# Value pages two per block, and the last sequence's early pages on a semaphore of their own

## What is computed

```
def paged(cache_l):
    rows = cache_l[page_table]
    return rows.reshape((n_seq, n_pages * cache_l.shape[1]) + cache_l.shape[2:])
past = (paged(cache_moba_k[l]), paged(cache_moba_v[l]), paged(cache_fox_k[l]), paged(cache_fox_v[l]), paged(cache_fox_logf[l]), state_hgrn[l])
...
p = jax.nn.softmax(s.reshape(B, H, qb, -1), axis=-1).reshape(s.shape)
return jnp.einsum('bhqnk,bhqnkd->bhqd', p.astype(vs.dtype), vs)
```

## Time and profile before

| | us |
|---|---|
| time, median of 3 executions | 1693.34 |
| lowest and highest of them | 1688.63, 1697.64 |
| profiled execution: span from first to last instruction | 1707.6 |
| TensorE busy in it | 1613.0 |
| POOL busy in it | 181.4 |
| TensorE's waits in line 1924 for key pages | 20.3 |

### The profile page before, as it was taken

One profiled execution on the slowest core, in us unless ns is written; L12 is line 12 of the kernel. 1 busy time (PEld: TensorE's weight loads), 2 busy tenths in 40 slices (PEclk: granted clock), 3 DMA queues, 4 the chain that ended last, 5 costly groups with the idle time before them and its releaser, 6 DMA issues. The chain is left out here.

```text
span 1707.6 us, 35370 instructions
## 1 busy us (share of the span) xinstructions
PE 1613.0 (94%) x13333; PEld 1498.8 (88%) x13333; DVE 1042.5 (61%) x1768; ACT 674.3 (39%) x987; POOL 181.4 (11%) x345
## 2 busy tenths in 40 slices
PE   6999999999898699999999999999898878999998
PEld 6999999976676599999999999999566657999997
DVE  6666557766485566665566665566656735666654
ACT  4333333445453553333343333425555444433322
POOL 0000000022454100000000000000235520000000
PEclk9999999999898899999999999999899988999999
DMA  6444446556677444444444444654677863544444
GB/s 200 149 150 152 152 137 146 127 179 221 208 240 235 146 149 150 150 155 138 148 156 151 153 142 141 161 136 125 214 221 228 257 202 94 180 147 147 141 146 138
DMA packets 282235, 282.34 MB, mean 165 GB/s; under 512 B 43022, under 2 KB 271046, under 8 KB 281990
## 3 DMA queue, kind: packets, MB, share of 16 engines
q1 hardware_dynamic: 266338, 234.28, 44.9%
q0 software_dynamic: 14464, 46.48, 8.5%
q10 hardware_dynamic: 1316, 0.03, 0.1%
HBM read 274.34 MB, written 6.40 MB: 164 GB/s over the span
## 5 line engine op out<-in xcount | busy, mean ns | idle before, releaser
L1707 PE MATMUL PS<-xh,whi 128*128 128x320 f32 x1840 | 576.1, 313 | 13.5 <-DVE xl L1021 7.3
L1707 PE MATMUL PS<-xl,whi 128*128 128x320 f32 x1840 | 569.4, 309 | 0.0
L1707 PE MATMUL PS<-xh,wlo 128*128 128x320 f32 x1840 | 569.3, 309 | 0.0
L687 ACT ACTIVATE whi<-raw 128x2048 fp32r<-128x2048 f32 (+1 forms) x181 | 330.9, 1829 | 565.1 <-PE PS L1707 560.2
L1012 DVE TENSOR_TENSOR wlo<-raw,whi 128x2048 fp32r<-128x2048 f32 (+1 forms) x181 | 395.2, 2185 | 237.2 <-ACT whi L687 235.5
L1707 PEld LDWEIGHTS PS<-xh,whi 128*128 128x128 f32 x1840 | 346.3, 188 | 16.7 <-DVE wlo L1012 10.7
L1707 PEld LDWEIGHTS PS<-xh,wlo 128*128 128x128 f32 x1840 | 346.2, 188 | 1.5
L1707 PEld LDWEIGHTS PS<-xl,whi 128*128 128x128 f32 x1840 | 346.1, 188 | 0.0
L1707 PE MATMUL PS<-hh,whi 128*128 128x320 f32 x704 | 217.7, 309 | 0.0
L1707 PE MATMUL PS<-hl,whi 128*128 128x320 f32 x704 | 217.5, 309 | 0.0
L1707 PE MATMUL PS<-hh,wlo 128*128 128x320 f32 x704 | 217.5, 309 | 0.0
(11 more groups left out here) (271 smaller groups left out, 1842.0 us busy)
## 6 DMA issues: line engine op xcount, KB each, us to landing
raw<-in_ffn_w_gate SPq DMA_DIRECT2D x45, 1024.0 KB
raw<-in_ffn_w_up SPq DMA_DIRECT2D x45, 1024.0 KB
raw<-in_ffn_w_down SPq DMA_DIRECT2D x32, 1024.0 KB
key_pages<-in_cache_moba_k SPq DMA_DIRECT2D x128, 192.0 KB, 3.2
raw<-in_w_in SPq DMA_DIRECT2D x46, 512.0 KB
value_pages<-in_cache_moba_v POOLq DMA_DIRECT2D x118, 192.0 KB, 3.6
key_pages<-in_cache_fox_k SPq DMA_DIRECT2D x128, 160.0 KB, 4.1
value_pages<-in_cache_fox_v POOLq DMA_DIRECT2D x118, 160.0 KB, 4.3
```

Of the source, the lines that this page charges most:

```text
L687: act.activation(whi[s][:, 0:nk, 0:w], raw[s][:, 0:nk, 0:w], ACT.Copy).then_inc(hi_done[s], 1)
L1707: last = te.matmul(out, w[wslot][r, kt, cols], x[r, at, :], start=start and n == 0 and m == 0, stop=stop and n == len(ktiles) - 1 and m == 2)
```

## The change

Value pages are issued in other blocks, in the same queue and with the same transfers.

- Sequence 0: pages 0 and 1 are issued behind `add_past(3)` and `add_past(4)`, before the loop; the other six in the loop's steps 2, 3 and 4, two each. Before, all eight were issued ahead of the loop, with `add_past(2)` to `add_past(5)` between them.
- Sequences 1 to 6: two pages in each of the steps 4q + 1 to 4q + 4. Before, four pages in each of the steps 4q + 2 and 4q + 3.
- The five early pages of sequence 7: one in each of the steps 11 to 15, on the new semaphore `late_values_in`. Before, three in step 24 and two in step 25, on `v_in`.
- `values(7)` waits for all five at once; `values(q)` of the others counts only its own loads.

```diff
+        late_values_in = sem("late_values_in")
...
-                        load_page(DB - 1, pg, late_pages[:, pg, :], v_in[pg])
+                        load_page(DB - 1, pg, late_pages[:, pg, :], late_values_in)
...
-                for i, first, count in ((2, 0, 1), (3, 1, 1), (4, 2, 2), (5, 4, 2)):
+                add_past(2)
+                add_past(3)
+                for i, first, count in ((4, 0, 1), (5, 1, 1)):
                     load_values(0, first, count)
                     add_past(i)
-                load_values(0, 6, 2)
                 pool.memset(a_blocks[:, :, :], 0.0).then_inc(products_cleared, 1)
                 for i in range(BLOCKS):
                     q, n = divmod(i, NBLK)
...
-                    if n >= 2 and 1 <= q < DB - 1:
-                        load_values(q, 4 * (n - 2), 4)
-                    if n < 2 and q == DB - 2:
-                        load_late_values(3 * n, 3 - n)
+                    if 2 <= i < 5:
+                        load_values(0, 2 * i - 2, 2)
+                    if NBLK < i <= NBLK * (DB - 1):
+                        load_values((i - 1) // NBLK, 2 * ((i - 1) % NBLK), 2)
+                    if NH <= i < NH + LATE:
+                        load_late_values(i - NH, 1)
                     if n == 2 and q == DB - 1:
                         load_values(q, LATE, NPG - LATE)
...
+                    if q == DB - 1:
+                        te.wait_ge(late_values_in, (L + 1) * LATE * 32)
                     for pg in range(NPG):
                         late = q == DB - 1 and pg < LATE
                         page = (late_pages if late else value_pages)[:, pg, :]
-                        loads = min(q + 2, DB) if pg < LATE and q >= DB - 3 else q + 1
-                        te.wait_ge(v_in[pg], (L * DB + loads) * 32)
+                        if not late:
+                            te.wait_ge(v_in[pg], (L * (DB - 1 if pg < LATE else DB) + q + 1) * 32)
```

## The result

The changed kernel takes 1680.97 us in the median of 5 runs (1677.13 to 1681.54), the kernel before beside it 1696.41 (1688.63 to 1697.64): a ratio of 0.9895, 95% interval 0.9869 to 0.9921. It is faster, by that ratio by 17.8 us (13.4 to 22.2); the two medians lie 15.4 apart. The prediction said 29 and 1664 us. The time lies outside the forecast's own range, 1652 to 1676, and on rival 1's 1681. When the same kernel was run again (experiment 11), the ratio was 0.9896 (0.9869 to 0.9923).

What follows compares the result with a forecast made beforehand. TensorE was held in both layers' attention stages by late value pages in block 26 and by key pages. Terms 12.9 + 6.6 + 10 + 2.5 - 2 - 1 = 29 us off the median 1693.34 gave 1664 us, range 1652 to 1676.

Steps and rivals of the forecast that it cites:

- rival 1: The bytes only move: block 26's stall goes, its slow clock and the start's key waits stay; 1681 us, chance 0.20.
- Late pages, own semaphore: Block 26, both layers: sequence 5's value products no longer wait for sequence 7's early pages; 12.9 us of stall gained.
- 3.3 a layer since the clock was full before the stall: Behind block 26's stall, TensorE's clock returns to its upper level; 6.6 us gained in all, bounds 0 and 9.4.
- The start: First five blocks: spreading sequence 0's value pages shortens key waits and a clock loss; 10 us gained, bounds 0 and 18.
- All terms are waits that both have, so I take them off the median: The profiled span, 1707.6 us, was 14 above the median; the 29 us were taken off the median, 1693.34.
- Layer 1, blocks 20 and 21: Two pages in place of four ahead of POOL's level logs end a 2.24 us wait; 2.5 us gained, bounds 0 and 3.5.
- Late pages and POOL's head of the line: Late pages delay block 14's keys, -2 us; POOL waiting to overwrite pages delays `add_past`, tightest at sequence 3, -1 us.
- Rival 2: Sequence 5's own pages are as late as the late ones were; only 3 to 6 us gained, 1689 us, chance 0.11.
- rival 3: POOL's wait makes `add_past(4q + 5)` late twelve times in two layers; slower, 1728 us, chance 0.06.

Runs made afterwards that it cites:

- experiment 11: The changed kernel run again unchanged, giving its second profiled execution: 1684.89 us, ratio 0.9896 to the kernel before.
- experiment 7: The changed kernel with the five late pages back in blocks 24 and 25, ahead of what else these issue: 1689.78 us, ratio 0.9937 to the kernel before.
- experiment 8: As experiment 7, but in block 24 sequence 5's last two value pages go ahead of the three late ones: 1684.58 us, ratio 0.99 to the kernel before.
- experiment 3: The kernel before with only sequence 0's value pages spread as in the change, no new semaphore: 1698.37 us, ratio 0.9999.
- experiment 6: The changed kernel with sequence 0's value pages issued as in the kernel before: 1686.34 us, ratio 0.9908 to the kernel before.
- the second look: The kernel before, unchanged, run for a second profiled execution: 1696.92 us in one run, span 1695.2.
- experiment 1: The kernel before with only the late pages' own semaphore, all pages issued where they were: 1681.5 us, ratio 0.9899.
- experiment 2: The kernel before with the own semaphore and late pages in blocks 11 to 15, other pages four per block as before: 1688.06 us, ratio 0.994.
- experiment 10: The kernel before with the own semaphore and late pages in blocks 12, 13, 16, 17 and 20, which issue no other value pages: 1683.03 us, ratio 0.9894.
- experiment 4: The kernel before with sequence 0 spread and two pages per block, late pages in blocks 24 and 25 on the old semaphore: 1697.45 us, ratio 0.9988.
- experiment 9: The changed kernel with the late pages one per block in blocks 20 to 24: 1680.43 us, ratio 0.9891 to the kernel before.

## Why the prediction was right in sign and too large

**Late pages, own semaphore: right in place, the stall right in size, the clock sized on one execution.** Taken were 6.4 + 6.5 us of stall and 6.6 of clock, 19.5. The pair of executions gave 6.40 + 6.51 and 6.8, 19.7 in all. Over all profiled executions block 26 takes 38.1 us in the four on the shared count (mean of 40.0, 37.3, 36.5, 38.8) and 22.3 in the nine on the own one (without experiment 7): 15.9 us. Of these 12.2 are stall (from the scores to the end of the products 19.5 and 7.3 us) and 3.7 are what stands behind it (18.6 and 14.9). So "3.3 a layer since the clock was full before the stall" is nearly twice what came in the mean: behind the products a layer takes 5.71 us where the clock holds, and up to 9.91 (experiment 8) where it falls without the stall.

**The start: the step that failed.** "I take 10 us, a little over half" was sized on the 11.9 us of waits and 6 of clock of one execution, in which blocks 0 to 4 took 28.3 and 30.4 us. The pair gave 11.5. But over the executions the old start takes 51.4 us (mean of seven, 48.7 to 58.7) and the spread one 47.4 (mean of seven, 45.4 to 49.4), 4.1 apart, and blocks 5 to 11 give 1.3 of it back (93.9 and 95.2). Some 3 us are left, and the runs of experiments 3 and 6 find 0 and 2.

**"All terms are waits that both have, so I take them off the median": wrong for this term.** The profiled execution stood 14 us above the median, and 7.5 us of that were in blocks 0 to 4: the second look had 51.2 there, at a span of 1695.2. What this profile had above the median was, by more than half, in a wait that was counted. Against its own span the sum seems to hold, 29 predicted and 28.7 measured, but that is in part luck: 31.2 us came where 29.5 were taken (block 26 and the start), 4.3 for 2.5 in blocks 20 to 22, 2.4 were gained in blocks 12 to 19 where 3 were to be lost, and some 9 that no term counts were lost, 4.8 of them in blocks 5 to 11.

**Layer 1, blocks 20 and 21: the number came, not by the reason given.** 2.5 us taken, 4.2 by the means (38.8 in both looks at before, 34.6 in both at the changed kernel). The prediction put the wait down to the burst of four pages ahead of the log. Experiments 1, 2 and 10 have four pages there too, and 35.0, 34.5 and 35.5 us. What both looks at before have is POOL's stop of 2.49 us within that burst, at the 206th transfer; in both looks at the changed kernel it stands at the 184th (2.40 us), in another block. Experiments 3 and 4 have it at the 206th too and wait there 0.69 us and not at all, so the stop alone does not make the whole wait. That the change moves the stop was not foreseen: the number is luck.

**Late pages and POOL's head of the line: right in sign, the first reason not seen.** -3 us taken; by the means of blocks 12 to 19, 101.8 in the four executions with four pages per block and late pages at 24 (98.7 to 106.8), 105.7 in the three with the changed order there (104.4 to 106.5), -3.9, within the spread of the first four. The waits for keys in block 12, which were to grow, are 4.4 us in the mean of the four and 3.8 in that of the three. The head of the line was seen: in layer 1 `add_past(17)` ended just before TensorE's turn, which had stood 0.54 us for it, after POOL's stop of 2.40 us within a page. Experiment 6 has this wait too (0.55 us), the second look at the changed kernel has none. POOL, then TensorE:

```profile
1283.64 0.54 POOL L630 DMA_DIRECT2D value_pages<-in_cache_fox_v  x1 [2.40 <-issue]
...
1287.70 0.20 POOL L624 COPY key_pages<-past 128x10 f32<-128x10 f32 x1
```

```profile
1288.04 1.62 PE L1928 MATMUL PS<-K,key_pages 128*128 128x128 f32 x12 [0.54 <-POOL key_pages L624]
```

**The sum, by the means:** 15.9 + 4.1 - 1.3 + 4.2 - 3.9 = 19.0, less 1.0 in blocks 27 to 30, is 18.0, against 17.8 measured. So close an agreement is luck: the two looks at each kernel alone differ by 24.1 us in blocks 0 to 30, and one look at a kernel differs from the next by up to 12.4.

**The rivals.** Rival 1's time, 1681 us, is the one measured, and much of its mechanism: moving the start's pages is worth 0 to 3 us, and of the clock behind block 26 about half stays (14.9 us behind the products in the two layers, where 11.4 would be had with the clock held and 18.6 were). The rule of the Trainium skill that stood with it ("DMA: Bandwidth & Descriptors", section "Issuing engines are not separate DMA queues"), by which spreading moves contention and removes none, left 19 us; experiments 3 and 4, at 0.9999 and 0.9988, agree with it within their intervals. Rival 2 is refuted for this change by 3.63 us in block 26 (in experiment 7's order it came true), rival 3 by one wait of 0.54 us where it wanted twelve of over 2.

**What the change is, then.** The semaphore is the whole gain that the runs can tell (0.9899 alone in experiment 1, 0.9895 with the rest). The two moves of pages cancel by the times: late pages in blocks 11 to 15 lose some 7 us beside four value pages per block (experiment 2) and none beside two; two per block lose some 7 us beside late pages in block 24 (experiment 7) and none without. The second of these is explained: late pages out of block 24 free sequence 5's last pages, which two per block put there (experiments 7 and 8). The first is not: the wait shown in experiment 2 stands in the changed kernel too.

## What to carry to other kernels

A count that two streams of transfers share makes the reader of the one wait for the other; look for a wait whose count takes in loads that the reader doesn't use, since a semaphore of its own was worth 17 us here and moved no transfer. Pages issued a few per block are spread only if the issuing engine isn't held by a buffer's release: look at the time stamps of the issue, not at the loop. And before sizing a wait from one profiled execution that stands above the median, take a second one and see whether the wait itself is what the first has too much of.

## What the runs showed of the hardware

**The granted clock falls in stretches in which TensorE waits for nothing.** Two windows of the changed kernel, layer 0, in block 7 (408.86 to 416.62 us):

```profile
411.00:414.00 3.00, 3.00 (x12) 1.54 (x11) 2.31 (x10) 0.49 (x1) 1.35 (x3) 0.82 0.88 251
414.00:417.00 3.00, 3.00 (x21) 2.67 (x24) 1.01 (x3) 0.87 (x2) 0.20 (x1) 0.61 0.52 192
```

TensorE is busy 3.00 of 3.00 us in both, and the clock is at its upper level for only a part of them. Each such dip made a block of 5 to 11 some 1.6 us longer (block 7: 7.76 us in place of 6.14); in 16 of the 28 passes through these blocks there was one or more, and TensorE's timeline shows no wait there in any of them. What sets them off is open. An execution has none to three of them in a layer's blocks 5 to 11, so they are part of the difference between executions.

**Such a dip is not always lost.** In the six passes with a dip in block 10 (10.4 to 10.5 us in place of 8.9) block 12 took 4.1 us in the mean, in the other 22 6.9: the likely reason, argued and not tested, is that the keys come in their own time and TensorE has used up 1.6 us of the wait for them.

**A level log of POOL holds up a small operation of VectorE to its own end.** The operation of line 1396 in experiment 2 took 2.12 us; clear of POOL it takes 0.22 (experiment 9, layer 1):

```profile
1280.13 0.22 DVE L1399 TENSOR_SCALAR gate_bias<-gate_sums 64x4 f32<-64x4 f32 x1
```

The Trainium skill ("SBUF — State Buffer", section "Who interferes with whom") says that VectorE and GpSimd share one pair of ports as an exclusive lock: where a VectorE operation uses that pair, whoever issues first holds it for the whole instruction and the other stands. In the four executions that have such an operation, it ends 0.03 or 0.04 us behind the log (465.55 and 465.52 here, 463.76 and 463.73 in experiment 11, 1284.29 and 1284.26 in experiment 7, 462.88 and 462.84 in experiment 9), which agrees with it. The order of issue is less clear: VectorE's start is shown 0.29 and 0.20 us ahead of the log's in the first two and 0.37 and 0.36 us behind it in the others.

**POOL's issue stops twice in an execution, at transfers that repeat.** Within a page, between its two transfers, POOL stands for more than 0.7 us only twice among the 256 transfers of value pages, in each of the 14 profiled executions. The first stop is at the 114th transfer in all of them (1.78 to 2.39 us). The second (2.13 to 2.49 us) depends on the kernel: the 206th in both looks at before and in experiments 3 and 4, the 184th in both looks at the changed kernel and in experiment 6, the 220th in experiments 1, 7 and 8, and others in the rest. What sets its place is open; experiment 1 issues the pages in the order of before and has it elsewhere. In the kernel before it stands ahead of the log that block 21 of layer 1 waits for, in the changed kernel's first look ahead of `add_past(17)`.
